# Expert rows of V summed on TensorE through weighted diagonals, rows dealt to two engines stage by stage, and the context projections placed between two choices

## The chip, the cores and the metric

The kernel runs on one core of one Trainium2 chip, in one launch. The metric is the device time in microseconds (us). Its engines here: TensorE (PE, with its weight loads PEld), VectorE (DVE), ScalarE (ACT), GpSimd (POOL) and SyncE (SP), and 16 DMA engines that both SP's and POOL's transfers share. Everything is in float32.

## What is computed

Two blocks follow each other on 256 tokens of width 1024, batch 1. The first has two layers (one with windowed and dilated attention, one with latent attention) and ends in a norm. The second has two layers with a context stream of 256 tokens beside the tokens. Each layer has a mixer (differential attention, a pooling branch, a convolution branch, gates, an output projection) and then a PEER expert layer:

```python
q = (xc @ w_q).reshape(PEER_CHUNK, PEER_HEADS, 2, PEER_HALF)
s = jnp.einsum('thid,hikd->thik', q, sub_keys)
s1, i1 = top_k(s[:, :, 0], 16); s2, i2 = top_k(s[:, :, 1], 16)
cand = s1[..., :, None] + s2[..., None, :]          # 256 candidates per head
top_s, pos = top_k(cand, 16)                         # 16 experts per head, 8 heads
gate = softmax(top_s)
u = u_emb[eidx]                                      # 128 rows of 1024 per token
hid = gelu(einsum('td,thkd->thk', xc, u))
wgt = gate * hid
out = einsum('thk,thkd->td', wgt, v_emb[eidx])
```

For each token 128 experts are chosen, and each needs a row of U (a dot product with the token) and a row of V (summed with a weight). The expert layer runs three times: for the context in layer 0, for the tokens in layer 0, for the tokens in layer 1. In the last layer the context only gives keys and values, so it has no expert layer there.

## The kernel before

Tokens lie on the 128 partitions, in two tiles t = 0, 1. The stages follow each other through `RUN`: run 0 is the context in layer 0, run 1 the tokens in layer 0, run 3 the context in layer 1 (keys and values only), run 2 the tokens in layer 1. The order of work is: `mixer(0)`, the choices of run 0 (`peer_front`), `first_block()` (which needs nothing of run 0), `mixer(1)`, choices of run 1, `mixer(3)`, `mixer(2)`, choices of run 2, end. `mixer(1)` reads the keys and values of the context, which don't depend on run 0's expert layer; `mixer(3)` needs the context after run 0's expert layer; `mixer(2)` needs the tokens after run 1's.

**The rows.** A work item is one expert number k of one tile: POOL issues one indirect DMA (line 974) that fetches for each of the 128 tokens its own row of 1024 floats, 524,288 bytes in all, into one of NG = 8 slots of `ring`. Items are in one fixed order: for each run and tile 128 of U, 128 of V and one with the gate row of the modulation (line 987). Item m waits until item m - 8 was used (`slot_used`). VectorE uses all of them: line 1325 for a U row (multiply with the token, sum into `hid`), lines 1328 and 1331 for a V row (`acc` = row times weight + `acc`, each waiting for the one before), lines 1335 and 1338 for the gate row and the sum into `H`.

**When VectorE takes rows.** `D_` (from line 1340) wraps VectorE's ordinary instructions: after each it adds `PACE[stage]` to an account and takes a row when the account is at 1. `beside(n)` takes `n * PER_PRODUCT[stage]` rows at a place where VectorE is about to wait for TensorE. `expert_rows` takes only rows that may be taken: U rows whose experts are chosen, V rows whose weights are made. `gelu_first` takes the last U rows of a tile and makes the argument of an exp, ScalarE takes the exp (`gelu_exp`, line 1013), `gelu_last` makes the weights. `TURN_AT` says at which place in the stages that is done for run 0: tile 0 after `norm("c")`, tile 1 after the pooling branch of `mixer(1)`.

**A choice.** `choose(r, t, g)` (four groups g for each tile) is 45 VectorE instructions that end in 32 expert numbers for each token (line 1840). `peer_front` of VectorE makes all eight groups of both tiles, then the softmax of the gates. POOL waits for a group's numbers before it fetches its U rows. Only after that do the last rows, weights and sums of both tiles follow.

**TensorE** runs its instructions strictly in the order written: projections (`tokens`, `columns`, line 420 in `sumk`), and `attention`, which goes over units (8 in each layer of the first block, 16 in a mixer), with scores of unit u, then transposed probabilities and values of unit u - 2. Its eight PSUM banks are handed out in rotation by `rot`; in `attention` four are for scores and four rotate. Weights come in blocks of 1 MB (1024 x 256 floats) through `wring`, four slots, fetched by SP (line 937).

## Time and profile before

| | us |
|---|---|
| median of 3 runs | 3917.76 (3910.81 to 3925.49) |
| profiled execution, its own time | 3921.26 |
| span of the profiled execution | 3919.5 |
| busy: PE / DVE / ACT / POOL | 1918.4 / 2800.7 / 402.3 / 1865.8 |

The span runs from the first to the last instruction. Busy time of an engine is the sum of its instructions; its share says nothing about whether the engine sets the end in a stage. A line of a windows view is one stretch of the span with each engine's busy time and count of instructions, the mean clock that TensorE was granted (1.00 is 2.4 GHz, 0.50 is 1.2 GHz), the mean busy share of the 16 DMA engines (it can come out a little above 1) and the gigabytes per second that they moved. Milestones that cut the span into stages: run 0's choices start at about 520, the attention of the first layer lies at 768 to 833, that of the second at 977 to 1033, that of `mixer(1)` at 1244 to 1366, run 1's choices begin at 1742, its last row is added at 2616, `mixer(2)` lasts until 3085, and the rest is run 2's expert layer.

### The profile page before, as it was taken

The page shows a single profiled execution, that of the slowest core. Times are in us where ns is not written, and L with a number is a line of the kernel's source. Part 1 is how long each engine was busy: PE and PEld are TensorE (multiplying, and loading weights), DVE is VectorE, ACT ScalarE, POOL GpSimd, SP SyncE. Part 2 cuts the span into 40 slices and gives each one's busy share as a digit, 9 for nine tenths or more (in the row PEclk, how much of TensorE's full clock was granted, in tenths as well). Part 3 has the DMA queues.
Part 4 walks back from the last instruction along what each step waited for, and adds up shares of the span by engine and source line. Part 5 has one row for each costly group of instructions (what it writes and reads, how often), then busy time and mean ns, then how long its engine had stood idle before and what let it go on. Part 6 is the DMA issues. An engine that isn't in the chain of part 4 may idle for free.

```text
span 3919.5 us, 27161 instructions
## 1 busy us (share of the span) xinstructions
PE 1918.4 (49%) x8842; PEld 1226.2 (31%) x8842; DVE 2800.7 (71%) x4787; ACT 402.3 (10%) x917; POOL 1865.8 (48%) x1556
## 2 busy tenths in 40 slices
PE   6899995386885698790014000029899800000000
PEld 3558484354532346470002000014475700000000
DVE  2322279945869977769997988975411699998898
ACT  1310110023211210010000000002300100000000
POOL 0000023423636766627746777740000377577776
PEclk8999997588786699995557555559999955555555
DMA  6744489967889899979859999963144588699999
GB/s 206 247 172 161 172 285 385 351 233 259 291 313 345 305 352 388 399 249 322 281 172 381 371 355 363 373 243 139 66 149 166 204 290 283 236 378 359 380 374 345
DMA packets 402329, 1111.67 MB, mean 284 GB/s; under 512 B 37139, under 2 KB 91603, under 8 KB 401420
## 3 DMA queue, kind: packets, MB, share of 16 engines
q0 software_dynamic: 223024, 811.71, 56.4%
q1 hardware_dynamic: 179164, 298.22, 21.7%
q8 instruction: 71, 1.16, 0.1%
q14 instruction: 70, 0.57, 0.0%
HBM read 1105.52 MB, written 4.29 MB: 283 GB/s over the span
## 4 chain that ended last, share of the span: by engine, by line
DVE 39%; PE 34%; POOL 12%; issue 8%; DMA 5%; ACT 2%; DVEq 0%; SPq 0%; ACTq 0%; POOLq 0%
PE PS L420 31%; DVE acc L1331 12%; DVE ring L1325 12%; POOL ring L974 12%; DMA wring<-in_w_in 2%; DVE work L1778 1%; DVE work L1775 1%; DVE work L1776 1%; DVE work L1385 1%; DMA ring<-in_peer_u,eidx 1%; ACT work L1001 1%; DVE work L1388 1%; DMA ring<-in_peer_v,eidx 1%; DVE work L1834 1%; DVE work L1837 1%
## 5 line engine op out<-in xcount | busy, mean ns | idle before, releaser
L974 POOL DMA_INDIRECT ring<-in_peer_u,eidx x768 | 955.4, 1244 | 1290.1 <-DVE eidx L1840 516.1
L974 POOL DMA_INDIRECT ring<-in_peer_v,eidx x768 | 900.4, 1172 | 605.0 <-DVE acc L1331 214.1
L1331 DVE SCALAR_TENSOR_TENSOR acc<-ring,small,acc 128x1024 f32<-128x1024 f32 x762 | 977.4, 1283 | 89.6 <-DMA ring<-in_peer_v,eidx 26.5
L1325 DVE SCALAR_TENSOR_TENSOR ring<-ring,xn_peer 128x1024 f32<-128x1024 f32 x768 | 932.5, 1217 | 86.2 <-DMA ring<-in_peer_u,eidx 79.3
L420 PE MATMUL PS<-wring,xnT 128*128 128x512 f32 (+2 forms) x1728 | 743.5, 592 | 22.6 <-issue 17.8
L420 PE MATMUL PS<-xnT,wring 128*128 128x128 f32 (+1 forms) x2896 | 481.9, 329 | 23.6 <-DMA wring<-in_w_in 12.9
L428 PE MATMUL PS<-const,work 128*128 128x128 f32 (+1 forms) x358 | 58.6, 329 | 870.8 <-DVE work L1388 850.8
L420 PEld LDWEIGHTS PS<-wring,xnT 128*128 128x128 f32 x1728 | 332.6, 196 | 426.1 <-issue 418.4
L420 PEld LDWEIGHTS PS<-xnT,wring 128*128 128x128 f32 x2896 | 438.6, 194 | 66.0 <-DMA wring<-in_w_in 14.8
L428 PEld LDWEIGHTS PS<-const,work 128*128 128x128 f32 (+1 forms) x358 | 50.8, 167 | 880.9 <-DVE work L1388 855.1
L1001 ACT ACTIVATE work<-PS 128x512 f32<-128x512 f32 (+5 forms) x377 | 189.0, 525 | 1096.0 <-PE PS L420 774.5
L420 PE MATMUL PS<-wring,work 128*128 128x512 f32 (+2 forms) x640 | 260.3, 567 | 30.4 <-DMA wring<-in_w_out 20.6
L1385 DVE TENSOR_TENSOR work<-work 128x512 f32<-128x512 f32 (+1 forms) x112 | 88.0, 786 | 248.1 <-ACT work L1075 124.6
L420 PEld LDWEIGHTS PS<-wring,work 128*128 128x128 f32 x640 | 123.1, 194 | 163.3 <-issue 144.4
L1385 DVE TENSOR_TENSOR work<-PS,work 128x512 f32<-128x512 f32 x32 | 22.1, 689 | 173.7 <-PE PS L420 147.3
L420 PE MATMUL PS<-work 128*128 128x128 f32 (+1 forms) x512 | 99.9, 358 | 73.2 <-ACT work L1001 73.2
L1385 DVE TENSOR_TENSOR work<-PS,rows 128x512 f32<-128x512 f32 x24 | 16.6, 692 | 160.3 <-PE PS L420 160.2
L491 PE MATMUL PS<-wring,cT 128*32 128x128 f32 x1536 | 69.9, 357 | 99.0 <-issue 99.0
L420 PEld LDWEIGHTS PS<-work 128*128 128x128 f32 x512 | 87.9, 259 | 89.8 <-ACT work L1001 89.8
L1687 DVE TENSOR_REDUCE small<-PS 128x2 f32<-128x1024 f32 (+1 forms) x48 | 50.2, 1045 | 69.9 <-PE PS L671 69.4
L491 PEld LDWEIGHTS PS<-wring,cT 128*32 128x32 f32 x1536 | 61.5, 146 | 109.3 <-issue 109.2
L1013 ACT ACTIVATE small<-small 128x128 f32<-128x128 f32 x6 | 1.9, 311 | 704.5 <-DVE small L1397 704.4
(163 smaller groups left out, 1499.8 us busy)
## 6 DMA issues: line engine op xcount, KB each, us to landing
wring<-in_w_in SPq DMA_DIRECT2D x128, 1024.0 KB, 6.1
wring<-in_w_mod SPq DMA_DIRECT2D x48, 1024.0 KB, 12.4
wring<-in_peer_wq SPq DMA_DIRECT2D x24, 1024.0 KB, 5.2
wring<-in_ab_w_in SPq DMA_DIRECT2D x13, 1024.0 KB, 22.2
wring<-in_conv_out_w SPq DMA_DIRECT2D x12, 1024.0 KB, 5.0
wring<-in_w_out SPq DMA_DIRECT2D x12, 1024.0 KB, 11.2
ring<-in_peer_u,eidx POOLq DMA_INDIRECT x768, 6.2
ring<-in_peer_v,eidx POOLq DMA_INDIRECT x768, 6.1
```

What stands on the lines that cost most here:

```text
L420: ins = pe.matmul(o, a, b, start=(i == 0), stop=(i == n - 1))
L428: ins = pe.transpose(PS[0:width, b, j * P:(j + 1) * P], src[:, (g + j) * width:(g + j + 1) * width], ident)
L491: pe.matmul(strips[j], cT[:, kk, :], w(kk, j * P, (j + 1) * P), start=(kk == 0), stop=False)
L974: pool.indirect_dma_start(ring[:, m % NG, :], None, table, bass.IndirectOffsetOnAxis(ap=eidx[:, r % 2, t, k:k + 1], axis=0))\
L1001: A(act.activation(dst, src, ACT.Copy), *tag)
L1325: v.scalar_tensor_tensor(out=slot, in0=slot, scalar=1.0, in1=xn_peer[:, t, :], op0=ALU.mult, op1=ALU.mult, accum_out=hid[:, k:k + 1]).then ...
L1331: v.scalar_tensor_tensor(out=acc[:, :], in0=slot, scalar=wgt[:, k - NSEL:k - NSEL + 1], in1=acc[:, :], op0=ALU.mult, op1=ALU.add).then_inc ...
L1385: D_(v.tensor_tensor(o, a, b, ALU.mult), *tag)
L1388: D_(v.tensor_tensor(o, a, b, ALU.add), *tag)
L1687: D_(v.tensor_reduce(nmax[:, u % 2, 0:2], PS[:, b:b + 2, 0:nk], AX_X, ALU.max, negate=True))
L1775: D_(v.max_index(idx[:, 0:8], vals[:, 0:8], src))
L1776: D_(v.match_replace(scratch, vals[:, 0:8], src, -3e38))
```

## The change

- 576 of the 768 V rows go to TensorE (`summed`): all of tile 0 in the three runs, and in tile 1 of runs 1 and 2 the rows with k % 4 != 3. VectorE keeps all 768 U rows, all V rows of run 0's tile 1, and one in four of the other tile 1's.
- For each such row ScalarE writes a 128 x 128 matrix `diag` with the tokens' weights on its diagonal (identity times a weight per partition; ND = 5 buffers), and TensorE multiplies it with the row in the ring, two matmuls of 512 columns that accumulate in two PSUM banks (6, 7 for tile 0; 4, 5 for tile 1). `slot_summed` counts them; POOL waits for the one or the other count. In an attention, TensorE sums a unit's rows after the values of unit u - 2 (`sum_rows`), and ScalarE writes their diagonals ahead of that unit's other work (`diags`); in runs 1 and 2 the sums stand after `mixer(3)` and after `peer_front(2)`. In tile 1 of these runs VectorE adds TensorE's sum to `acc` once, before the gate row.
- The order of the items is written out (`ITEMS`): run 0 has V rows of tile 0 in the attention of the first and of the second layer (5 per unit, 40 each) and 48 in that of `mixer(1)` (3 per unit), with 50 and 78 U rows of tile 1 between; in runs 1 and 2 the last 80 V rows of tile 0 alternate with U rows of tile 1.
- The weights of run 0's tile 0 are made before the first attention (`TURN_AT` "ab"), those of its tile 1 before the attention of `mixer(1)` ("heads 1"). `rows_upto` makes VectorE finish rows up to an item at a place; `rows_free` lets it take rows up to an item from there on.
- In runs 1 and 2 tile 0 is chosen, finished with its U rows and weighed before tile 1 is chosen; in run 1 `mixer(3)` stands between the choice of tile 0 and its weights.
- Paces change: "front0" 0.3 to 0.35, "front1" and "front2" 0.5 to 0.35, 16 rows per product in "m3"; none while the second tile of runs 1 and 2 is chosen. The eight rows before the first choice and the rows beside the output projection are gone.
- While TensorE sums, fewer banks rotate: [4, 5] in the attention with sums, six after those of the first block. `hid` and `wgt` get one copy per tile.

```diff
-PACE = {"front0": 0.3, "ab": 0.8, "c": 0.8, "m1": 0.7, "front1": 0.5, "m3": 0.8, "front2": 0.5}
-PER_PRODUCT = {"ab": 6, "c": 6, "m1": 5, "m3": 4}
-BESIDE_QUERIES = 8
+PACE = {"front0": 0.35, "ab": 0.8, "c": 0.8, "m1": 0.7, "m3": 0.8, "front1": 0.35, "front2": 0.35}
+PER_PRODUCT = {"ab": 6, "c": 6, "m1": 5, "m3": 16}
+SUMS_PER_UNIT = {"ab": 5, "c": 5, 1: 3}
+        def items(r, kind, t, first=0, last=NSEL):
+            ITEMS.extend((r, kind, t, k) for k in range(first, last))
+        def both(r, t, first):
+            for k in range(first, NSEL):
+                items(r, "v", 0, k, k + 1)
+                items(r, "u", 1, k - first, k - first + 1)
+            items(r, "u", 1, NSEL - first)
+        a, b = len(range(8)) * SUMS_PER_UNIT["ab"], 16 * SUMS_PER_UNIT["ab"]
+        U1_EARLY = 50
+        items(0, "u", 0)
+        items(0, "v", 0, 0, a)
+        items(0, "u", 1, 0, U1_EARLY)
+        items(0, "v", 0, a, b)
+        items(0, "u", 1, U1_EARLY)
+        items(0, "v", 0, b)
+        items(0, "gate", 0, 0, 1)
+        items(0, "v", 1)
+        items(0, "gate", 1, 0, 1)
+        for r in (1, 2):
+            items(r, "u", 0)
+            items(r, "v", 0, 0, 48)
+            both(r, 1, 48)
+            items(r, "gate", 0, 0, 1)
+            items(r, "v", 1)
+            items(r, "gate", 1, 0, 1)
+        def summed(r, kind, t, k):
+            return kind == "v" and (r > 0 or t == 0) and (t == 0 or k % 4 != 3)
+        PE_ITEMS = [m for m, it in enumerate(ITEMS) if summed(*it)]
+        DVE_ITEMS = [m for m, it in enumerate(ITEMS) if not summed(*it)]
+        ORDER = {m: (summed(*ITEMS[m]), n) for own in (PE_ITEMS, DVE_ITEMS) for n, m in enumerate(own)}
+        PLACE = {it: ORDER[m][1] for m, it in enumerate(ITEMS)}
+        SUMS = {(r, t): [k for k in range(NSEL) if summed(r, "v", t, k)] for r in range(3) for t in range(T)}
+        OWN = {(r, t): [k for k in range(NSEL) if not summed(r, "v", t, k)] for r in range(3) for t in range(T)}
+        def used_wait(m):
+            by_pe, n = ORDER[m]
+            return slot_summed if by_pe else slot_used, n + 1
...
+                state["banks"] = [4, 5] if s in SUMS_PER_UNIT else [4, 5, 6, 7]
                 for u in range(len(units) + 2):
                     if u < len(units):
                         take([2 * (u % 2), 2 * (u % 2) + 1], ("S", s, u))
@@ -470,7 +517,25 @@
                     if u > 1:
                         turns(u - 2)
                         values(u - 2)
-                state["banks"] = 8
+                    if u < len(units):
+                        sum_rows(SUMS_PER_UNIT.get(s, 0))
+                state["banks"] = list(range(6)) if s in ("ab", "c") else list(range(8))
+            def sum_rows(n):
+                for _ in range(n):
+                    m = PE_ITEMS[state["summed"]]
+                    r, _, t, k = ITEMS[m]
+                    b, _ = sums(r, t)
+                    if k == 0:
+                        take([b, b + 1], ("acc", r, t))
+                    pe.wait_ge(*at("diag", r, t, k))
+                    pe.wait_ge(g_landed[m % NG], 16 * (m // NG + 1))
+                    for c in range(2):
+                        ins = pe.matmul(PS[:, b + c, :], diag[:, state["summed"] % ND, :], ring[:, m % NG, 512 * c:512 * c + 512],
+                                        start=(k == SUMS[r, t][0]), stop=(k == SUMS[r, t][-1]))
+                    ins.then_inc(slot_summed, 1)
+                    state["summed"] += 1
...
+            for m, (r, kind, t, k) in enumerate(ITEMS):
+                if m >= NG:
+                    pool.wait_ge(*used_wait(m - NG))
+                if kind == "gate":
                     _, layer, which = modrow(r)
...
+            def diags(n):
+                for _ in range(n):
+                    j = weighted["next"]
+                    r, _, t, k = ITEMS[PE_ITEMS[j]]
+                    if k == 0:
+                        act.wait_ge(*at("weights_of", r, t))
+                    if j >= ND:
+                        act.wait_ge(slot_summed, j - ND + 1)
+                    A(act.activation(diag[:, j % ND, :], ident, ACT.Copy, scale=wgt[:, t, k:k + 1]), "diag", r, t, k)
+                    weighted["next"] += 1
             def root(dst, src, waits, *tag):
                 act.wait_ge(*at(*waits))
...
-            top_exps(1)
+            top_exp(1, 0)
+            mixer(3, [("experts", 1, 0, GROUPS - 1), ("h_peer", 0, T - 1)])
             gelu_exp(1, 0)
-            mixer(3, [("experts", 1, T - 1, GROUPS - 1), ("h_peer", 0, T - 1)])
+            diags(len(SUMS[1, 0]))
+            top_exp(1, 1)
             gelu_exp(1, 1)
+            diags(len(SUMS[1, 1]))
             mixer(2, [("tok", "k", 3, T - 1), ("h_peer", 1, T - 1)])
             peer_front(2)
-            top_exps(2)
             for t in range(T):
...
+                        v.wait_ge(slot_used, j)
+                        total = acc[:, :]
+                        if SUMS[r, t]:
+                            total = sums(r, t)[1]
+                            v.wait_ge(slot_summed, PLACE[r, "v", t, SUMS[r, t][-1]] + 1)
+                        if SUMS[r, t] and OWN[r, t]:
+                            v.tensor_tensor(acc[:, :], acc[:, :], total, ALU.add).then_inc(*step("dve"))
+                            v.wait_ge(L.sem["dve"], L.count["dve"])
+                            total = acc[:, :]
+                        v.tensor_tensor(acc[:, :], total, slot, ALU.mult).then_inc(slot_used, 1)
...
+            def rows_upto(r, kind, t, k):
+                rows_at["upto"] = PLACE[r, kind, t, k] + 1
+                expert_rows(rows_at["upto"] - rows_at["next"])
+                assert rows_at["next"] == rows_at["upto"], (r, kind, t, k, rows_at)
+            def rows_free(r, kind, t, k):
+                rows_at["upto"] = PLACE[r, kind, t, k] + 1
...
+            def weigh(r, t):
+                gelu_first(r, t)
+                top_scale(r, t)
+                gelu_last(r, t)
...
+            mixed_norm(0, [])
+            rows_free(0, "u", 0, NSEL - 1)
+            for t in range(T):
+                choose_tile(0, t, norm_ab)
+            for t in range(T):
+                top_scale(0, t)
             first_block()
             pace("m1")
             mixer(1, [("product", "oT", "c", T - 1, 1)])
             pace("front1")
-            peer_front(1, [("product", "xnT", ("p", 0), T - 1, 1)])
-            expert_rows(2 * NI * T)
+            mixed_norm(1, [("product", "xnT", ("p", 0), T - 1, 1)])
+            rows_upto(0, "gate", 1, 0)
+            rows_free(1, "u", 0, NSEL - 1)
+            choose_tile(1, 0)
+            top_scale(1, 0)
+            pace("m3")
+            mixer(3, [("product", "xnT", ("m", 1), T - 1, 1)])
+            pace(None)
             gelu_first(1, 0)
             gelu_last(1, 0)
-            pace("m3")
-            mixer(3, [("product", "xnT", ("m", 1), T - 1, 1)])
-            expert_rows(NI * T)
-            gelu_first(1, 1)
-            gelu_last(1, 1)
-            expert_rows(NI * T)
-            pace(None)
+            choose_tile(1, 1)
+            weigh(1, 1)
+            rows_upto(1, "gate", 1, 0)
             mixer(2, [("product", "xnT", ("m", 3), T - 1, 1)])
             pace("front2")
-            peer_front(2, [("product", "xnT", ("p", 1), T - 1, 1)])
-            for t in range(T):
-                expert_rows(NI * T)
-                gelu_first(2, t)
-                gelu_last(2, t)
-            expert_rows(NI * T)
+            mixed_norm(2, [("product", "xnT", ("p", 1), T - 1, 1)])
+            rows_free(2, "u", 0, NSEL - 1)
+            choose_tile(2, 0)
+            weigh(2, 0)
+            pace(None)
+            choose_tile(2, 1)
+            weigh(2, 1)
+            rows_upto(2, "gate", 1, 0)
     return L.mark
```

## Rows read from the trace of the kernel before

**Rows 1.** The page's slices, 40 of 98 us; PEclk and DMA in tenths.
```profile
DVE  2322279945869977769997988975411699998898
PEclk8999997588786699995557555559999955555555
DMA  6744489967889899979859999963144588699999
```

**Rows 2.** Windows of five long stages; columns: busy us of each engine (count), clock, DMA share, GB/s.
```profile
0.00:520.00 520.00, 457.92 (x2455) 285.61 (x2456) 139.97 (x297) 84.28 (x204) 6.49 (x14) 0.96 0.55 186
520.00:1742.00 1222.00, 893.89 (x4019) 580.95 (x4018) 953.86 (x1661) 199.45 (x477) 624.36 (x514) 0.80 0.89 326
1742.00:2616.00 874.00, 92.13 (x421) 58.94 (x419) 783.21 (x1293) 25.11 (x42) 624.72 (x514) 0.55 0.89 327
2616.00:3085.00 469.00, 434.89 (x1601) 261.39 (x1601) 158.09 (x274) 84.37 (x180) 0.00 (x0) 0.97 0.36 122
3085.00:3919.50 834.50, 39.53 (x354) 39.34 (x352) 765.60 (x1265) 9.10 (x16) 610.25 (x514) 0.53 0.89 327
```

**Rows 3.** Windows: a V phase, a U phase of run 2, V rows beside mixer(3).
```profile
3371.00:3548.50 177.50, 0.00 (x0) 0.00 (x0) 164.07 (x129) 0.00 (x0) 137.82 (x126) 0.50 0.96 362
3551.00:3731.00 180.00, 0.00 (x0) 0.00 (x0) 157.51 (x257) 0.00 (x0) 141.29 (x128) 0.50 0.98 371
2042.00:2246.00 204.00, 59.98 (x149) 27.38 (x147) 172.92 (x142) 12.21 (x19) 148.09 (x126) 0.64 0.97 365
```

**Rows 4.** Groups by line in that V phase: busy us, mean ns, idle before.
```profile
L1331 DVE SCALAR_TENSOR_TENSOR acc<-ring,small,acc 128x1024 f32<-128x1024 f32 x116 | 149.0, 1284 | 12.1
L974 POOL DMA_INDIRECT ring<-in_peer_v,eidx x115 | 125.4, 1091 | 35.7 <-issue 34.7 <-DVE acc L1331 0.9
```

**Rows 5.** POOL's timeline at the end of the U phase: start, duration, idle before.
```profile
3726.74 0.98 POOL L974 DMA_INDIRECT ring<-in_peer_v,eidx  x1 [0.30 <-issue]
3728.02 0.97 POOL L974 DMA_INDIRECT ring<-in_peer_v,eidx  x1 [0.30 <-issue]
```

**Rows 6.** Windows: one group's choice, the rest of the choices, before a first choice.
```profile
3184.60:3226.10 41.50, 0.00 (x0) 0.00 (x0) 40.71 (x110) 0.00 (x0) 32.47 (x23) 0.50 0.83 281
3226.00:3370.00 144.00, 0.00 (x0) 0.00 (x0) 138.91 (x392) 0.93 (x3) 90.97 (x62) 0.50 0.69 230
1742.00:1754.00 12.00, 12.00 (x110) 12.00 (x109) 11.14 (x32) 1.79 (x3) 0.00 (x1) 1.00 0.65 186
```

**Rows 7.** Groups by line of VectorE in that group's choice.
```profile
L1325 DVE SCALAR_TENSOR_TENSOR ring<-ring,xn_peer 128x1024 f32<-128x1024 f32 x23 | 27.9, 1211 | 0.0
L1325 DVE DVE_READ_ACCUMULATOR ring<-ring,xn_peer 128x1 f32 x23 | 1.9, 83 | 0.0
```

**Rows 8.** TensorE: 64 matmuls of 512 columns at the high clock, from the timeline.
```profile
866.61 27.70 PE L420 MATMUL PS<-wring,work 128*128 128x512 f32 x64 [1.00 <-ACT work L1001]
```

**Rows 9.** Windows: choices, attention, after it, attention, stages, attention, rest of mixer(1).
```profile
520.00:768.00 248.00, 147.84 (x1440) 123.82 (x1438) 233.50 (x657) 19.53 (x43) 100.63 (x106) 0.73 1.02 375
768.00:833.00 65.00, 38.20 (x193) 32.24 (x194) 52.65 (x102) 22.94 (x81) 38.18 (x31) 0.61 1.00 347
833.00:921.00 88.00, 74.14 (x224) 40.14 (x223) 15.33 (x28) 16.23 (x32) 0.94 (x1) 0.94 0.29 98
977.00:1033.00 56.00, 40.74 (x181) 36.13 (x182) 46.44 (x58) 21.24 (x69) 33.24 (x26) 0.62 0.79 257
1033.00:1244.00 211.00, 161.66 (x392) 74.38 (x390) 169.62 (x183) 26.15 (x46) 109.06 (x90) 0.85 0.90 335
1244.00:1366.00 122.00, 71.00 (x240) 41.80 (x240) 118.18 (x232) 35.04 (x94) 95.42 (x73) 0.60 0.89 306
1366.00:1742.00 376.00, 325.35 (x1206) 208.45 (x1206) 273.83 (x342) 35.00 (x58) 211.81 (x163) 0.93 0.94 350
```

**Rows 10.** The same two stages in mixer(2), where no rows run beside.
```profile
2720.00:2780.00 60.00, 45.61 (x234) 26.64 (x235) 45.93 (x93) 34.81 (x93) 0.00 (x0) 0.91 0.04 15
2780.00:3077.00 297.00, 288.41 (x1057) 182.60 (x1057) 61.05 (x97) 30.50 (x53) 0.00 (x0) 1.00 0.42 141
```

**Rows 11.** U rows of VectorE in the choices of run 0 (two records each).
```profile
520.00:768.00 248.00, 119.59 (x197) 0.73 1.02 375
```

**Rows 12.** ScalarE on 128 x 128, from the timeline.
```profile
3731.97 0.31 ACT L1013 ACTIVATE small<-small 128x128 f32<-128x128 f32 x1 [362.75 <-DVE small L1397]
```

More of the change, by code:

```diff
@@ L964, in _ @@
             pool.wait_ge(mod_stored, 64)
-            def rows_in(r, t, table, kinds):
-                for k in range(NSEL):
-                    m = item(r, t, kinds * NSEL + k)
-                    if not kinds and k % (NSEL // GROUPS) == 0:
-                        pool.wait_ge(*at("experts", r, t, k // (NSEL // GROUPS)))
-                    if m >= NG:
-                        pool.wait_ge(slot_used, m - NG + 1)
-                    pool.indirect_dma_start(ring[:, m % NG, :], None, table,
-                                            bass.IndirectOffsetOnAxis(ap=eidx[:, r % 2, t, k:k + 1], axis=0))\
-                        .then_inc(g_landed[m % NG], 16)
-            for r in range(3):
-                for t in range(T):
-                    rows_in(r, t, DR["peer_u_2"].rearrange("l e d -> (l e) d"), 0)
-                    rows_in(r, t, DR["peer_v_2"].rearrange("l e d -> (l e) d"), 1)
-                    m = item(r, t, 2 * NSEL)
-                    pool.wait_ge(slot_used, m - NG + 1)
+            tables = {"u": DR["peer_u_2"].rearrange("l e d -> (l e) d"), "v": DR["peer_v_2"].rearrange("l e d -> (l e) d")}
+            for m, (r, kind, t, k) in enumerate(ITEMS):
+                if m >= NG:
+                    pool.wait_ge(*used_wait(m - NG))
+                if kind == "gate":
                     _, layer, which = modrow(r)
@@ L988, in _ @@
                         .then_inc(g_landed[m % NG], 16)
+                    continue
+                if kind == "u" and k % (NSEL // GROUPS) == 0:
+                    pool.wait_ge(*at("experts", r, t, k // (NSEL // GROUPS)))
+                pool.indirect_dma_start(ring[:, m % NG, :], None, tables[kind],
+                                        bass.IndirectOffsetOnAxis(ap=eidx[:, r % 2, t, k:k + 1], axis=0))\
+                    .then_inc(g_landed[m % NG], 16)
         @block.scalar
@@ L1201, in mixer @@
                     return
+                turn(f"heads {r}")
                 for u in range(len(M_UNITS) + 2):
+                    if u < len(M_UNITS):
+                        diags(SUMS_PER_UNIT.get(r, 0))
                     if r == 0 and u and u % 2 == 0:
@@ L1303, in _ @@
             for t in range(T):
+                top_exp(2, t)
                 gelu_exp(2, t)
+                diags(len(SUMS[2, t]))
+            assert weighted["next"] == len(PE_ITEMS)
         @block.vector
         def _(v):
-            rows_at = {"next": 0, "chosen": 0, "weighted": 0, "pace": 0.0, "due": 0.0, "per_product": 0}
+            rows_at = {"next": 0, "chosen": 0, "weighted": 0, "pace": 0.0, "due": 0.0, "per_product": 0, "upto": len(DVE_ITEMS)}
             def expert_rows(n):
@@ L1315, in expert_rows @@
                 for _ in range(n):
-                    m = rows_at["next"]
-                    if m >= min(rows_at["chosen"], rows_at["weighted"] * NI + NSEL):
+                    j = rows_at["next"]
+                    if j >= rows_at["upto"]:
+                        return
+                    m = DVE_ITEMS[j]
+                    r, kind, t, k = ITEMS[m]
+                    if kind == "u" and j >= rows_at["chosen"] or kind == "v" and r * T + t >= rows_at["weighted"]:
                         return
@@ L1682, in mixer @@
                     return
+                turn_to_v(f"heads {r}")
                 for u in range(len(M_UNITS) + 1):
@@ L1699, in mixer @@
                 v.wait_ge(*at("read", "O", r, len(M_UNITS) - 1))
+                if r == 1:
+                    rows_upto(0, "gate", 0, 0)
+                    rows_free(0, "gate", 1, 0)
                 for t in range(T):
@@ L1784, in mixed_norm @@
                 v.wait_ge(*row_wait(f"m2_{r}"))
+                assert rows_at["next"] > (PLACE[r - 1, "u", 1, NSEL - 1] if r else -1)
                 for t in range(T):
                     for n in range(2):
-                        beside(0.5)
                         v.wait_ge(*at("product", "wo", r, t, n))
@@ L1867, in _ @@
             pace("front0")
-            peer_front(0, [], norm_ab)
+            mixed_norm(0, [])
+            rows_free(0, "u", 0, NSEL - 1)
+            for t in range(T):
+                choose_tile(0, t, norm_ab)
+            for t in range(T):
+                top_scale(0, t)
             first_block()
```

124 lines of the change are left out of this document (66 added, 58 removed).

## The prediction

> **What bounds the kernel now.** I read the slices of the page first, then windows by long stage, then each stage's own. VectorE is busiest in the sum, 2800.7 us, but the slices show three kinds of stage [rows 1]. In `mixer(0)` and `mixer(2)` TensorE works at its high clock and the DMA engines are half idle. In the two long stretches from 1742 to 2616 and from 3085 to the end TensorE is all but idle, VectorE is near full and so are the DMA engines. Between 520 and 1742 all three share the work. The stages last 520, 1222, 874, 469 and 834.5 us [rows 2]; the DMA share is 0.55, 0.89, 0.89, 0.36 and 0.89.
>
> In the row stretches the question is which of three is late: VectorE, POOL that issues, or the transfers. A V phase takes 177.5 us for 128 rows, 1.387 us each, a U phase 180, 1.406 us [rows 3]. In the V phase VectorE's instruction takes 1.284 us with 0.104 (12.1 / 116) before it, its wait on its own last sum; POOL takes 1.091 and 0.30 of issue, which is the same 1.39; the DMA share is 0.96 to 0.98 [rows 3, 4]. So all three run in step there, and the U phase shows that the transfers don't come faster where VectorE could take more: its pair of instructions is 1.211 + 0.083 = 1.294 us [rows 7] against 1.406 spent. I take 1.40 us per row as the price of a row's transfer. Taking V rows from VectorE gives nothing in such a phase. What can be had is the time in which the channel doesn't run full. While VectorE chooses experts, a group of 41.5 us holds 23 rows, one each 1.80 us (share 0.83), and the rest of the choices, after the 128 U rows of tile 0 are used up, falls to 0.69 [rows 6]: V rows can't start, because no weights are made before all choices of both tiles are.
>
> **The change, part by part.** The sum is made against the profiled execution.
>
> *Work moved.* 576 V rows leave VectorE: 576 x 1.39 = 800 us of its time, most of it beside transfers that stay. TensorE gets 1152 matmuls of 512 columns: at the high clock 27.70 / 64 = 0.433 us each [rows 8], 0.87 a row; at the low clock, half of it, twice that, 1.73 a row. The first is under the 1.40 of a transfer, the second over it. ScalarE's diagonal is near 0.31 us [rows 12], bounds 0.31 and 0.60 (a 512-column copy would be the upper neighbour), below 1.40 either way, so hidden; five buffers let it run ahead.
>
> *Run 2, the tail (834.5 us).* VectorE's cost of one group's choice without rows is 41.5 - 23 x 1.294 = 11.7 us [rows 6, 7]. After: 10 us until the first group's numbers (12 in run 1 [rows 6]); three more groups with 45 x 0.35 = 16 rows each, 3 x (11.7 + 16 x 1.294) = 97; 3 for the softmax's shift. By then 48 rows are used and 8 are in the ring. From there the channel runs full: 72 U rows of tile 0 and 386 items behind them, 458 x 1.40 = 641 us. The second choice, 4 x 11.7 = 47 us, lies beside V rows that TensorE sums, and 47 / 1.40 = 34 rows is less than the 48 that stand before the first U row of tile 1. If TensorE is at the low clock there, 27 rows pass instead of 34; that is 7 x 1.40 = 10, of which I take 8. The last tile ends with TensorE's sum added (1.2), gate and add: 5, and the store 4. Sum 10 + 97 + 3 + 641 + 8 + 5 + 4 = 768, so -66 (bounds -25, if a second choice stays as empty as the first, and -77, all that a share of 0.89 leaves to 0.98: 834.5 x 0.09 / 0.98). The two V phases of tile 1 stay at the transfer's pace: three rows of four on TensorE, 5.2 us even at the low clock, against 5.6 for the four transfers.
>
> *Run 1 (874 us).* The same with 12 for the first group and no store, and `mixer(3)` inside: its 60 us of TensorE lay beside V rows before too [rows 3]; its weights are 8 MB, that is 8.4 MB / 0.38 = 22 us of channel. It now lies beside the last U rows of tile 0 (64 of 72 by the two `beside` of 32), whose transfers take 101 us. VectorE's own part of it, two norms and one set of heads, some 25 us, is also beside them. 12 + 97 + 3 + 641 + 22 + 8 + 5 = 788, -86; but the share leaves no more than 874 x 0.09 / 0.98 = 80, so I take -80 (-30 to -86). `mixer(2)` starts only after the last sum, so this counts in full.
>
> *520 to 1742 (1222 us), run 0.* Here the rows are spread beside stages that have their own bounds, so each step is a difference:
> - Choices: 0.35 instead of 0.3 and no V or U row left for the attention. 99 U rows (197 records) were done [rows 11], now all 128 must be before the first attention: 29 x 1.294 = 38 less what the gaps hold, and the channel, already at 1.02 [rows 9], needs as much; with the weights' own 5, +33 (bounds +15, +45).
> - First attention: 65 us with 30 U rows on VectorE. Now 40 V rows: 32 to fetch and 8 of the next kind, 56 us, and what else was loaded, (347 x 65 - 31 x 524) / 380 = 16. I take 77, +12. TensorE's own 38 us at a clock of 0.61 and 40 x 0.87 to 1.73 make 73 to 107 if nothing overlaps: +8 to +42.
> - 833 to 977: 50 U rows instead of 28 V rows, but from the start, where the channel is at 0.29 and VectorE is busy 15 of 88 us [rows 9]. They wait ahead of the gates by six: +5 (0 to +15).
> - Second attention: 56 us, PE 40.7 at 0.62 with 26 rows. With 40 rows on TensorE I take +15 (0 to +50, as the first).
> - 1033 to 1244: 78 rows instead of 90 issued [rows 9]. 12 x 1.40 at a share of 0.90: -10 (-17 to +10; the weights of tile 1 now need its last U row here).
> - Attention of `mixer(1)`: 122 us, VectorE busy 118, 73 rows issued. Without rows the same stage takes 60 in `mixer(2)` [rows 10]. Three sums a unit add 48 x 0.87 = 42 at the high clock and 83 at the low: 102 to 143. TensorE busier than its 71 of 122 should be granted more than 0.60: I take 105, -17 (-20 to +21).
> - Rest of `mixer(1)`: 376 us with 163 rows at a share of 0.94. Some 40 of them are gone, 56 us of channel; TensorE's own need is 297 [rows 10], the channel's 0.94 x 376 - 56 = 297. Both at 297 together give some 328: -48 (-20 to -70). Banks 6 and 7 are asked for while the sum of tile 0 is unread, a few us in it.
> Sum +33 + 12 + 5 + 15 - 10 - 17 - 48 = -10, bounds by these -60 and +90.
>
> *The other stages* (520 and 469 us) hold no rows: 0. One fewer rotation bank pair in the first block's stages costs 0: copies of 0.6 us stand against products of 7.
>
> Total -10 - 80 - 66 = -156. The span of 3919.5 lies in an execution of 3921.3 (1.8 around it), 3.5 over the median of the runs: 3921.3 - 3.5 - 156 = 3762. I predict 3762 us.
>
> **What the skill says against the terms.** The row's transfer at 0.524 MB in 1.40 us is 374 GB/s, and 371 and 375 stand in the windows [rows 3, 9]. The Trainium skill, "DMA: Bandwidth & Descriptors", section "Where 436 GB/s comes from", has 358 GB/s as the bound for what comes from HBM: 1.46 us a row, which the trace already beats, so by that page 916 rows would cost 55 us more, 3817. The same page's table under "Measured (HBM→SBUF, 128 partitions, SWDGE, issued from GpSimd)" has 425 GB/s for one core alone, 1.23 us a row; it speaks for rival B. Of the clock the profile has 0.50 in all stretches with an idle TensorE, 0.64 where it is busy for 29 in 100 and 0.60 at 58 in 100, 1.00 where it is full [rows 3, 9, 10]; "TensorE: Matmul & The Clock Gate", section "HAM oscillation — how this bites in real kernels", says that waits for data between bursts throw it back to the low clock again and again. That is rival C.
>
> **Rivals.**
> A, slower than before: in run 0 TensorE runs in written order, so a V row that hasn't landed holds scores and transposes behind it, and ScalarE can't write the next diagonal, nor take its exps, until the sum is made. If none of the 128 rows in the attentions overlaps with the attention's own chain, they add 128 x 1.40 = 179 us at a full channel and nothing is saved on VectorE there; with the later stages delayed too by half of that (90) and the choices' 45, run 0 is at +314 against -146 from the later runs: about 4086. It decides from a loss of some 150 us in run 0, about half of that price. Against it: five transfers take 7 us and a unit already takes 8 [rows 9], so they fit beside each other.
> B, the gather speeds up once VectorE's chain of sums is gone: POOL shows spacings of 1.28 us (0.98 + 0.30) for a while [rows 5]. 916 rows x 0.12 = 110 us more: 3652. For it: V phases are at exactly VectorE's 1.388. Against: the U phase averages 1.406 with VectorE free for 1.294.
> C, the low clock holds in the phases of sums, with a wait of some 0.2 before each row: 1.9 us for each of the first 48 V rows, 0.5 too many, and 6.0 instead of 5.6 for each of 32 groups of four in tile 1, 2 x (24 + 13) = 74, and 60 from the upper bounds of the attentions: 3762 + 134 = 3896.
> D, only half of the idle channel is won: VectorE's waits on its own instructions are no longer hidden by a row beside them, and the pace of 0.35 leaves rows to later. Runs 1 and 2 give 73 instead of 146: 3835.
>
> **Chances.** Forecast (3720 to 3805) 0.52; B 0.12; C 0.10; D 0.18; A 0.08. The range: the forecast's own, most of D and part of B, 3685 to 3860. Within 0.5% (20 us) is what a measurement of this kernel can't tell from no change. Faster by more: 0.52 + 0.12 + 0.18 and 0.06 of C, 0.88; within: 0.05, the rest of C and a little of A; slower: 0.07, A.
>
> **What the profile after would show.** Right: the tail from the first choice about 768 us with the DMA share 0.95 or more in the second choice (before 0.69 to 0.83); run 1's stretch near 794; a V row's cadence in tile 1 still 1.39 to 1.40; the attention of `mixer(1)` near 105 us. Wrong: a V cadence of 1.27 (B), a clock of 0.50 with PE busy throughout a sum phase and DMA under 0.85 (C), attentions of the first block over 100 us with TensorE waiting for `ring` (A), a second choice with the channel idle (D).

## The result, and the profile after

| | us |
|---|---|
| median before (4 runs beside it) | 3916.49 (3910.81 to 3925.49) |
| median after, 4 runs | 3888.07 (3882.66 to 3892.66) |
| ratio, 95% interval | 0.9925, [0.9902, 0.9948] |
| profiled execution after, its span | 3886.7 |

The change makes the kernel 0.75% faster, 28 us where 156 were forecast, and the time lies above the range (3685 to 3860). The page after, its slices and the groups that changed (columns of the groups: busy us, mean ns, idle before and what ended it):

```profile
PE   6899995369897898899263875698899930587389
PEclk8999997589898899999676998799999975799789
DMA  6754479987768858984889999993144478999999
L535 PE MATMUL PS<-ring,diag 128*128 128x512 f32 x2304 | 1046.1, 603 | 521.8 <-ACT diag L1087 421.7
L1087 ACT ACTIVATE diag<-const,small 128x128 f32<-128x128 f32 x576 | 226.1, 402 | 797.8 <-PE PS L535 785.9
L1420 DVE SCALAR_TENSOR_TENSOR acc<-ring,small,acc 128x1024 f32<-128x1024 f32 x189 | 242.4, 1282 | 277.5 <-DMA ring<-in_peer_v,eidx 271.5
```

The count of the first group tells the error: 576 rows gave 2304 matmul records, four each and not two. Its mean of 603 ns is longer than the pace at which the records follow each other. The timeline of PE in an attention of the changed kernel shows that pace: five rows (20 records) in 8.85 us and one (4 records) in 1.88, some 0.44 to 0.47 us a record:

```profile
819.62 1.88 PE L535 MATMUL PS<-ring,diag 128*128 128x512 f32 x4
821.43 1.13 PE L602 MATMUL PS<-work 64*128 64x256 f32 x8
822.49 8.85 PE L535 MATMUL PS<-ring,diag 128*128 128x512 f32 x20
```

The long stages of the changed kernel as windows (columns as in [rows 2], which they answer to), cut at the same places of the code:

```profile
0.00:520.00 520.00, 458.34 (x2472) 287.80 (x2473) 141.32 (x303) 84.55 (x205) 6.49 (x14) 0.97 0.55 188
520.00:1833.00 1313.00, 1043.02 (x4412) 620.36 (x4410) 810.36 (x1527) 237.30 (x597) 596.07 (x514) 0.89 0.83 302
1833.00:2639.00 806.00, 516.64 (x1420) 237.47 (x1418) 510.22 (x1068) 115.25 (x268) 535.78 (x514) 0.85 0.94 357
2639.00:3108.00 469.00, 432.55 (x1603) 260.86 (x1604) 159.67 (x276) 84.50 (x180) 0.00 (x0) 0.97 0.36 122
3108.00:3886.70 778.70, 447.91 (x1248) 204.25 (x1246) 494.70 (x1042) 98.08 (x240) 531.66 (x514) 0.82 0.93 351
```

Run 0's stretch is 91 us longer (1313 for 1222), run 1's 68 shorter (806 for 874), the tail 56 shorter (778.7 for 834.5). In the stretch that grew, the DMA share fell from 0.89 to 0.83 and TensorE went from 894 to 1043 us at a clock of 0.89. Five of its parts, which answer to [rows 9], are shown (choices, first attention, second attention, attention of `mixer(1)`, rest of `mixer(1)`); the stages between them took 130 us (907 to 1037) and 201 (1138 to 1339):

```profile
520.00:806.00 286.00, 147.12 (x1415) 122.22 (x1413) 264.91 (x710) 19.12 (x41) 140.19 (x132) 0.72 1.00 370
806.00:907.00 101.00, 91.84 (x325) 47.08 (x326) 24.22 (x50) 35.59 (x118) 41.01 (x44) 0.96 0.84 283
1037.00:1138.00 101.00, 94.36 (x349) 53.59 (x348) 19.89 (x34) 38.92 (x121) 36.52 (x39) 1.00 0.68 231
1339.00:1473.00 134.00, 123.11 (x422) 58.47 (x421) 47.97 (x99) 48.30 (x137) 44.12 (x47) 0.99 0.55 177
1473.00:1833.00 360.00, 316.51 (x1121) 199.73 (x1119) 227.35 (x254) 31.57 (x55) 158.06 (x124) 0.94 0.82 305
```

In all three attentions PE is busy for 91 to 93% at a clock of 0.96 to 1.00, VectorE for 20 to 36%, and the DMA share is 0.84, 0.68 and 0.55: TensorE is the bound, not the rows. The waits of the first one say the same from POOL's side (engine and line waiting, for whom, total us, times, longest):

```profile
POOL ring L1047 <- PE PS L535: 58.4, 39, 5.7
ACT diag L1087 <- PE PS L535: 35.4, 29, 1.9
```

In the tail, the second choice, the phase behind it and the last V phase, which answer to [rows 6] and [rows 3]:

```profile
3346.00:3423.00 77.00, 76.39 (x173) 33.86 (x174) 70.88 (x251) 18.44 (x48) 41.23 (x42) 0.97 0.84 294
3423.00:3704.00 281.00, 163.94 (x340) 57.98 (x338) 158.92 (x261) 32.70 (x82) 213.94 (x212) 0.89 1.01 393
3708.00:3880.00 172.00, 168.30 (x384) 73.33 (x384) 44.17 (x36) 37.78 (x96) 120.47 (x122) 0.99 0.98 380
```

The second choice takes 77 us, not 47, and TensorE is busy in all of it with 173 / 4 = 43 rows, 1.73 us each in 75 of the 77. The last V phase is 172 us for 128 rows, 1.34 each, against 1.387 before.

What sets the pace of the phases with nothing but rows is read from POOL, which issues them. In the last V phase its lines are these:

```profile
L1047 POOL DMA_INDIRECT ring<-in_peer_v,eidx x121 | 119.9, 991 | 43.9 <-issue 32.6 <-PE PS L535 9.0 <-DVE acc L1432 2.2
```

It waited 11.2 us for a slot to come free, and for the rest issued one row after another, 0.99 us for the instruction and 0.30 between two, 1.30 in all, with the DMA share at 0.98. So POOL's issuing and the transfers are at their limit together, and no run tells whether the one holds back the other.

### The profile page after: what moved, and what is told of

Its sections match the earlier page's. It is cut to its first block, busy times and chain, and to the rows that moved or that the text cites. A ratio compares the mean times of both kernels' runs of the same rounds, so it can differ in the third digit from the quotient of the medians.

```text
span 3886.7 us, 31785 instructions
## 1 busy us (share of the span) xinstructions
PE 2898.5 (75%) x11146; PEld 1610.7 (41%) x11146; DVE 2116.3 (54%) x4213; ACT 619.7 (16%) x1489; POOL 1670.0 (43%) x1556
## 4 chain that ended last, share of the span: by engine, by line
PE 53%; POOL 14%; DVE 12%; DMA 11%; issue 7%; ACT 2%; SPq 0%; DVEq 0%; ACTq 0%; POOLq 0%
PE PS L467 30%; PE PS L535 19%; POOL ring L1047 14%; DVE ring L1414 5%; DMA ring<-in_peer_u,eidx 3%; DMA ring<-in_peer_v,eidx 3%; DMA wring<-in_w_mod 3%; DMA wring<-in_w_in 2%; ACT work L1062 1%; DVE work L1493 1%; PE PS L556 1%; PE PS L736 1%; DVE work L1891 1%; DVE work L1894 1%; DMA wring<-in_ab_w_in 1%
## 5 line engine op out<-in xcount | busy, mean ns | idle before, releaser
L1047 POOL DMA_INDIRECT ring<-in_peer_u,eidx x768 | 855.9, 1114 | 1541.1 <-DVE work L1891 489.3
L535 PE MATMUL PS<-ring,diag 128*128 128x512 f32 x2304 | 1046.1, 603 | 521.8 <-ACT diag L1087 421.7
L1047 POOL DMA_INDIRECT ring<-in_peer_v,eidx x768 | 804.1, 1047 | 515.5 <-PE PS L535 309.1
L535 PEld LDWEIGHTS PS<-ring,diag 128*128 128x128 f32 x2304 | 426.2, 192 | 1119.4 <-ACT diag L1087 629.3
L467 PE MATMUL PS<-xnT,wring 128*128 128x128 f32 (+1 forms) x2896 | 489.8, 332 | 39.8 <-DMA wring<-in_w_in 24.8
L1420 DVE SCALAR_TENSOR_TENSOR acc<-ring,small,acc 128x1024 f32<-128x1024 f32 x189 | 242.4, 1282 | 277.5 <-DMA ring<-in_peer_v,eidx 271.5
L1087 ACT ACTIVATE diag<-const,small 128x128 f32<-128x128 f32 x576 | 226.1, 402 | 797.8 <-PE PS L535 785.9
L467 PE MATMUL PS<-work 128*128 128x128 f32 (+1 forms) x512 | 72.4, 285 | 46.8 <-ACT work L1062 46.8
```

Source lines behind the costliest of these rows:

```text
L467: ins = pe.matmul(o, a, b, start=(i == 0), stop=(i == n - 1))
L535: ins = pe.matmul(PS[:, b + c, :], diag[:, state["summed"] % ND, :], ring[:, m % NG, 512 * c:512 * c + 512], start=(k == SUMS[r, t][0]), s ...
L1047: pool.indirect_dma_start(ring[:, m % NG, :], None, tables[kind], bass.IndirectOffsetOnAxis(ap=eidx[:, r % 2, t, k:k + 1], axis=0))\
L1087: A(act.activation(diag[:, j % ND, :], ident, ACT.Copy, scale=wgt[:, t, k:k + 1]), "diag", r, t, k)
L1420: v.scalar_tensor_tensor(out=acc[:, :], in0=slot, scalar=wgt[:, t, k:k + 1], in1=acc[:, :], op0=ALU.mult, op1=ALU.add).then_inc(slot_used, 1)
```

## Experiments

Times are medians of one job each with its interval against the runs of the kernel before in that job; three jobs ran on three chips (medians of before 3923, 3909 and 3911).

**Half of TensorE's price.** One of the two matmul calls for each row, two of its four records, except for the first and last row of a tile; what the kernel leaves out is half of the columns of the sums.

```diff
-                    for c in range(2):
+                    for c in range(2 if k in (SUMS[r, t][0], SUMS[r, t][-1]) else 1):
```

> The changed kernel, but of each V row that TensorE sums only the first half of the columns is multiplied (the first and the last row of a tile in full), so the second half of the sums is left out. Theory P (a V row costs TensorE four matmuls of 512 columns, 1.73 us at the high clock, and that lengthens run 0's attentions and holds rows back in the second choices): the two attentions of the first block fall from 101 us each to 70 to 80, that of mixer(1) from 134 to 105 to 115, the second choices let 55 rows pass instead of 44, and the median is 3775 to 3810. Theory W (TensorE stands waiting for the rows' transfers, or for ScalarE's diagonals): the attentions stay within 10 us, the median at 3865 to 3890.

Measured: 3869.25, ratio 0.9853 [0.9811, 0.9895], above the 3775 to 3810 expected. The first numbers of run 1 came at 1752.8, 91 us earlier than in the changed kernel (1844.2), so the stages behind had lost: its last V phase took 184 us, against 172. So I ran it again, on another chip, beside the changed kernel:

> The same kernel as e1_half (of each V row on TensorE only the first half of the columns, the second half of the sums is left out), now beside the changed kernel on one chip. Theory P: first choice of run 1 near 1753 and not 1845, and the whole faster than the changed kernel by that, 80 to 100 us: 3785 to 3815 if the later phases transfer alike. Theory G (what TensorE's price costs before 1845 is given back behind it, as e1_half's 3869 on another chip looks like): within 30 us of the changed kernel.

> The changed kernel unaltered, the measure for g1_half: 3880 to 3945, first choice of run 1 at 1845.

Measured: 3772.69, 0.9665 [0.9621, 0.9709], against 3894.13, 0.9956 [0.9931, 0.9980], for the changed kernel beside it: 121 us, more than the 80 to 100 expected. The windows of g1_half's three attentions:

```profile
801.00:876.00 75.00, 60.96 (x245) 31.71 (x246) 24.13 (x50) 34.70 (x118) 39.29 (x43) 0.92 1.00 359
1007.00:1078.00 71.00, 62.60 (x285) 40.03 (x283) 20.32 (x35) 39.19 (x123) 37.46 (x40) 1.00 0.90 334
1277.00:1373.00 96.00, 84.38 (x332) 41.33 (x330) 48.15 (x99) 47.43 (x138) 44.56 (x48) 0.98 0.76 252
```

And the first expert numbers of run 1, VectorE's timeline, in g1_half:

```profile
1741.69 0.18 DVE L1956 CAST eidx<-work 128x32 int32<-128x32 f32 x1
```

in the kernel as changed:

```profile
1844.18 0.18 DVE L1956 CAST eidx<-work 128x32 int32<-128x32 f32 x1
```

At half the price the attentions take 75, 71 and 96 us (forecast 77, 71, 105), and run 0 ends 12 us earlier than before (1753.5), where -10 was forecast. Theory W falls: ScalarE's diagonals, the code's waits and the rows' transfers were the same, and only the matmuls went. Theory G falls on this chip. Of rival A, a row not landed that holds TensorE, nothing is seen in the changed kernel's attentions: PE's waits there name no transfer of a row, and the channel was emptier than in g1_half, not fuller.

One edit, two chips: beside the kernel before, the half-priced kernel gained 54 us on the first (3923.36 to 3869.25) and 138 on the second (3910.76 to 3772.69). The last section comes back to that.

**Banks.** The kernel before with the change's fewer PSUM banks: `[4, 5]` in the attentions instead of four, six in the first block's stages instead of eight.

> The kernel before with only the PSUM banks of the change: two banks rotate instead of four in the attentions of the first block and of mixer(1), six instead of eight in the stages behind those of the first block. Theory P: within 10 us of before in each attention, median 3905 to 3930. Theory B (the fewer banks lengthen the attentions by holding a transpose until VectorE has read a value): the first block's attentions 15 us or more longer each, 3945 or more.

Measured: 3925.17, 0.9999 [0.9978, 1.0020]; the attentions 62.5, 56 and 123 us for 65, 56 and 122. Theory B falls, and the banks cost nothing, as taken.

**Run 0 as before, runs 1 and 2 as changed.**

```diff
-            return kind == "v" and (r > 0 or t == 0) and (t == 0 or k % 4 != 3)
+            return kind == "v" and r > 0 and (t == 0 or k % 4 != 3)
-SUMS_PER_UNIT = {"ab": 5, "c": 5, 1: 3}
+SUMS_PER_UNIT = {}
-TURN_AT = {"ab": (0, 0), "heads 1": (0, 1)}
+TURN_AT = {"c": (0, 0), "pooled 1": (0, 1)}
+        for t in range(T):
+            items(0, "u", t)
+            items(0, "v", t)
+            items(0, "gate", t, 0, 1)
...
```

> Run 0 as in the kernel before (all its V rows on VectorE, its order, paces and places), runs 1 and 2 as changed. Theory P, with the losses all in run 0 (+91 us until the first choice of run 1) and the gains in runs 1 and 2 (67 and 55): 3917 - 122, 3785 to 3805. Theory S (the stages are coupled, part of run 1's gain comes from rows that run 0 had finished early): 3820 to 3860.

> As e2_run0, but all V rows of runs 1 and 2 stay on VectorE too, which takes them at a pace of 0.5 during the second choice: the new order alone, no row on TensorE. Theory T (TensorE is needed, since only with it a row passes without VectorE's time in the second choice): a second choice takes 47 us plus some 90 rows of 1.39, 172 us for 126 us of transfers, 40 to 50 us lost in each run against e2_run0; median 3875 to 3895. Theory O (the order alone brings the gain): within 20 us of e2_run0.

Measured: 4181.39, 1.0633 [1.0587, 1.0680], and 4219.06, 1.0734 [1.0689, 1.0779]. Both were spoilt by my edit: after a tile's weights VectorE was not allowed any row of run 0 until the next forced place, and the first numbers of run 1 came at 2071, not at 1753.5. They say one thing: where rows are only taken at forced places, run 0 is 318 us longer. Mended (`rows_free(0, "gate", 1, 0)` after the weights of run 0):

> As e2_run0, which by an oversight took no rows of run 0 between its weights and the last stages; now VectorE is free to take them as in the kernel before. Theory P (all the loss in run 0, gains of 38 and 12 in runs 1 and 2 on the chip of e2_run0, 67 and 55 by the first profile of the changed kernel): 3790 to 3870, first choice of run 1 at 1745 to 1765 as before. Theory S (coupled stages): first choice of run 1 as before, but no gain behind it.

> The changed kernel again, unaltered, beside the others, as the measure for them. In its first profile the rows of the last V phase passed at 1.32 us each, while in e1_half and e2_run0, whose code for the last expert layer is the same or does less, they took 1.40. Theory X (the transfers' pace differs between executions or chips, whatever the kernel): tail from its first choice to the end 764 to 810, median 3880 to 3945, and rows of the last V phase at 1.32 to 1.40. Theory Y (the pace comes from the kernel: TensorE at 1.73 us a row holds the issue back just so far that the channel runs evenly): 1.32 again, median 3880 to 3895.

Measured: f2_run0 3805.97, 0.9724 [0.9688, 0.9759]; f1_after 3892.84, 0.9952 [0.9929, 0.9976]. The stages of f2_run0:

```profile
520.00:1740.00 1220.00, 889.47 (x4035) 576.80 (x4034) 953.98 (x1654) 199.85 (x477) 624.02 (x513) 0.82 0.90 327
1740.00:2546.50 806.50, 502.92 (x1271) 221.33 (x1270) 511.51 (x1070) 112.88 (x264) 546.46 (x514) 0.84 0.94 352
3013.00:3809.50 796.50, 449.54 (x1254) 205.37 (x1252) 495.36 (x1044) 98.03 (x240) 563.50 (x514) 0.82 0.93 343
```

Run 0's stretch is 1220 us, for 1222 before; run 1 keeps its 806. The tail is 796.5 us here and 778.7 in the changed kernel, by the phase that the last section takes up. The loss was in run 0 alone, and this version beats both kernels: 87 us under the changed one beside it, 103 under the one before. Run again on the third chip:

> f2_run0 unaltered, the measure for g3_second: 3795 to 3830, with the first choice of run 1 at 1750 to 1760.

Measured: 3795.63, 0.9726 [0.9677, 0.9775]; the first numbers of run 1 came at 1762.8, a little later than the 1750 to 1760 expected.

**Order without TensorE.** f2_run0 with all V rows on VectorE (`summed` returns False), which takes rows at a pace of 0.5 in the second choices.

> As f2_run0, with all V rows on VectorE: the order of runs 1 and 2 alone, mended as f2_run0. From e3_order's later stages (846 and 820 us for 862 and 820): 3890 to 3910. If TensorE's sums are what gains, f2_run0 is 30 to 40 us faster or more; if the order is, they are within 15 us.

Measured: 3873.09, 0.9903 [0.9868, 0.9938], faster than the 3890 to 3910 expected. So of the 103 us, 36 come from the order with this pace and 67 from TensorE's sums. Its second choice in the tail and its last V phase:

```profile
3294.00:3466.00 172.00, 0.00 (x0) 0.00 (x0) 168.66 (x365) 0.00 (x0) 93.00 (x91) 0.50 0.84 282
3687.00:3867.00 180.00, 0.00 (x0) 0.00 (x0) 165.86 (x130) 0.00 (x0) 133.56 (x122) 0.50 0.95 357
```

VectorE alone needs 172 us for a choice and 91 rows, as worked out in the expectation; theory O falls: the two are 67 us apart, and not within 15.

**The share in tile 1.** f2_run0 with `k % 2 == 1` instead of `k % 4 != 3` in tile 1.

> As f2_run0, but in tile 1 of runs 1 and 2 TensorE sums every second V row instead of three of four. Theory P (at 1.73 us a row three of four, 5.2 us in four transfers of 5.3 to 5.6, leave TensorE busy 98% and set the pace of that phase): 2 to 10 us faster than f2_run0, the V phases of tile 1 at 165 us or less. Theory C (the channel sets it): within 3 us of f2_run0 and 170 to 180 us.

Measured: 3807.13, 0.9735 [0.9699, 0.9772], the same as f2_run0. POOL's issues of a V phase of tile 1 spread over 170 us in run 1 and 181 in run 2, for 173 and 172 in f2_run0. TensorE, 98% busy there, was not what set the pace: the same follows from g1_half, where PE's busy time in the last V phase fell from 167 to 110 us and the phase only from 172 to 167. Theory P falls for this phase.

**Filling the second choice.** f2_run0; one V row in four of tile 0 stays on VectorE, at a pace of 0.11 in the second choice, and U rows of tile 1 begin behind 64 V rows.

> As f2_run0; besides, in tile 0 of runs 1 and 2 one V row in four stays on VectorE, which takes it during the second choice (pace 0.11), and U rows of tile 1 start behind 64 V rows instead of 48. Theory P (44 rows pass in a second choice of 77 us because TensorE needs 1.73 us for each, so 19 us of the channel are lost in each run): the second choice takes 90 to 105 us with 65 to 77 rows, 10 to 30 us faster than f2_run0, 3775 to 3800. Rival (the row on VectorE costs the choice as much as the channel wins): within 8 us of f2_run0.

Measured: 3810.71 (3784.26 to 3834.96), 0.9741 [0.9678, 0.9803], against 3795.63: unclear. The second choice and the phase behind it in the tail, g3_second:

```profile
3285.00:3388.00 103.00, 93.00 (x208) 38.74 (x206) 86.31 (x248) 21.03 (x53) 73.89 (x69) 0.98 0.96 356
3388.00:3656.00 268.00, 101.90 (x171) 36.48 (x172) 179.95 (x283) 16.93 (x44) 207.39 (x187) 0.73 0.97 363
```

and g4_run0:

```profile
3256.00:3337.00 81.00, 76.14 (x173) 33.70 (x174) 74.46 (x264) 18.75 (x48) 43.63 (x45) 0.94 0.85 301
3337.00:3620.00 283.00, 165.65 (x343) 58.81 (x342) 164.56 (x273) 34.62 (x88) 213.84 (x215) 0.89 1.01 398
```

The choice was filled as meant, 69 issues at a share of 0.96 for 45 at 0.85. Then the phase behind it ran at 363 GB/s instead of 398, and the sum of both is 371 us for 364. The profiled execution of g3_second is the slowest of its four (3834.96), and it was 8 us behind already at the first numbers of run 1 (1770.9 for 1762.8), and up to there the two kernels do the same. What sets that pace is open (below), so whether filling pays is too.

## Why the prediction was wrong

**The step that failed** is the first of the sum: "TensorE gets 1152 matmuls of 512 columns: at the high clock 27.70 / 64 = 0.433 us each [rows 8], 0.87 a row". The 0.433 is right, and it is the price of one *record*. The code behind that row is `sumk` over 8 k for two halves of the columns and two tiles, 32 calls, and the row has 64 records: a float32 matmul leaves two. I counted calls of the change and took the price of records. A row costs 4 x 0.433 = 1.73 us at the high clock, over the transfer's 1.40, not under it. The row alone could have told: [rows 8] has x64 for what is 32 calls in the kernel's code.

Point by point, against the forecast:

| step | forecast | after | g1_half (price 0.87) |
|---|---|---|---|
| until the first attention | +33 | +38 | +33 |
| first attention | +12 | +36 | +10 |
| stages | +5 | -14 | -13 |
| second attention | +15 | +45 | +15 |
| stages | -10 | -10 | -12 |
| attention of `mixer(1)` | -17 | +12 | -26 |
| rest until run 1's first experts | -48 | -16 | -19 |
| run 0 in all | -10 | +91 | -12 |

With the price as I had it, the model holds on that chip: g1_half's run 0, and its whole, 138 us under the kernel before where 156 were forecast (3773 against 3762; part of this nearness is that the kernel before ran 7 us faster there). The size of the mistake in time is the 121 us between it and the changed kernel on one chip. In the two profiled executions, which lie 138 us apart, 105 of them (1847.1 - 1741.7, the first numbers of run 1 in g2_after and g1_half) are in run 0.

The bounds of these terms (+42, +50, +21) held what was measured, since I had put the low clock's 1.73 there. The sum's upper bound did not: the upper bounds of the seven steps add up to +163, and I wrote +90, just under the +91 that came. Rival C's 3896 is only 8 us from the result, by luck: its clock was wrong in the attentions (0.96 to 1.00, where it wanted the low one), and 74 of its 134 us were to come from runs 1 and 2, which together fell only 22 short of the forecast.

**Rest of `mixer(1)`**: wrong even at the right price. I took channel and TensorE as evenly mixed, 297 us of either in 328. VectorE took the 128 V rows at once and the channel was full until the last one; the chain of waits of the changed kernel has stretches of TensorE behind weights there:

```profile
1589.98 28.19 DMA wring<-in_w_in
1618.22 10.03 PE PS L467 x32
1628.27 38.87 DMA wring<-in_w_in
```

These waits are only a part. In all of the 360 us PE waited 26.4 us for weights (1.8 in the stage of [rows 10], and 30.0 in this stage of the kernel before), and its own busy time was 316.5 us at a clock of 0.94, not 288.4 at 1.00. After 1727 the rows were over and the channel was half empty to the end of the stage:

```profile
1727.00:1833.00 106.00, 102.00 (x432) 60.84 (x430) 28.26 (x62) 15.10 (x28) 0.00 (x0) 1.00 0.48 169
```

**Run 1 (-80 forecast, -68) and the tail (-66, -56)** came nearly as reckoned, but partly because two errors are of opposite sign, which is luck. The second choice took 77 us for 47. My 11.7 us for a group's choice was too low: I subtracted 23 x 1.294 us of rows from 41.5, but records of VectorE overlap where they follow each other: in that window those of the rows last 29.8 us in sum and those of the choice itself 18.1 (64 records), in a busy time of 40.7. The latter last 72.0 / 4 = 18.0 us a group in the second choice of the changed kernel, where no row stands in the gaps. That is most of the 30 us; the engine stood idle for 6 of the 77, so rival D's reason, waits that a row no longer hides, was real but small. TensorE filled the stretch with 43 rows instead of my 34. Against it, row phases ran at 1.32 to 1.34 us a row instead of 1.40 where VectorE's chain of sums was gone: rival B was right in kind and gave half to two thirds of its 0.12, on this chip.

**The rules weighed in the prediction.** 358 GB/s as a bound from HBM ("DMA: Bandwidth & Descriptors", "Where 436 GB/s comes from" in the Trainium skill): windows of 393 and 398 GB/s in phases of nothing but rows beat it. The 425 of the same page was not reached either. The clock: in the three attentions PE was busy for 91 to 93% and was granted 0.96 to 1.00. The section "HAM oscillation — how this bites in real kernels" of "TensorE: Matmul & The Clock Gate" (the Trainium skill) tells of bursts of matmuls that are shorter than the wait for data behind each. The attentions are no such case, so they say nothing against it. Nearer to it are the phases of alternating rows, where PE waits for most rows. In the tail of the changed kernel it was granted 0.89 there, in g1_half, with half of the records, 0.58:

```profile
3330.00:3595.00 265.00, 141.04 (x152) 34.67 (x152) 152.99 (x251) 28.30 (x71) 204.03 (x202) 0.58 1.02 397
```

So waits between bursts can bring the low clock in this program, and need not. In g1_half it cost nothing that shows: the phase took 265 us for 281.

## What to carry to other kernels

Count an operation's cost in the records that the trace has for one call, not in calls: divide the count of a row by the calls of the code behind it before a duration is used. Work moved to an idle engine is free only in the stages where that engine is idle; here the same move gave 67 us in two stretches and, with its order, took 91 in a third, and dealing it by stage gave 2.7% instead of 0.75%. An instruction's cost from a mixed window is not the window less the sum of its neighbours' records, where records overlap. In `mixer(1)` the rows filled the channel first and left it half empty behind; that spreading them over the stage would have gained is likely, but no run tested it.

## What the runs showed of the hardware

A gather of 524,288 bytes has no one pace. In one execution of the changed kernel (f1_after) the two like phases, second tile's U rows with V rows on TensorE, ran so in run 1 and in run 2:

```profile
2190.00:2484.00 294.00, 160.41 (x326) 57.00 (x325) 161.54 (x267) 32.72 (x84) 225.30 (x210) 0.87 0.99 375
3446.00:3722.00 276.00, 161.14 (x334) 56.79 (x332) 161.91 (x268) 32.58 (x83) 207.59 (x213) 0.89 1.02 402
```

1.40 us per row in one, 1.30 in the other, with PE, VectorE and ScalarE busy for the same time. POOL was not: its instruction took longer, and only for V rows (the U rows' took 0.98 and 0.99 us). The lines of its V rows in the two phases:

```profile
L1047 POOL DMA_INDIRECT ring<-in_peer_v,eidx x84 | 102.0, 1214 | 28.3 <-PE PS L535 21.3 <-issue 7.0
L1047 POOL DMA_INDIRECT ring<-in_peer_v,eidx x85 | 81.6, 960 | 27.3 <-issue 24.1 <-PE PS L535 3.3
```

84 times 0.25 us is 21 us, more than the difference of 18. In f2_run0 it is the phase of run 2 that is slow (300 us) with V rows at 1.22 us of POOL, so it does not belong to the rows that one run reads. Whether POOL's instruction held the transfers back or they it, is not shown.

The other difference is between chips. The same half-priced kernel had a median of 3869.25 on one and 3772.69 on another, and the four executions on each lie within 14 us. Its last V phase, in e1_half and in g1_half:

```profile
3673.00:3857.00 184.00, 118.17 (x196) 35.21 (x196) 48.40 (x45) 37.86 (x97) 125.12 (x126) 0.90 0.96 365
3601.00:3768.00 167.00, 110.04 (x195) 31.47 (x193) 44.08 (x35) 36.53 (x91) 118.61 (x122) 0.96 0.98 385
```

In e2_run0, on the chip of e1_half, that phase took 183 us. So theory Y falls, though f1_after by itself came out as it said (3892.84, and 1.32 in the last V phase). Of theory X it is left that the pace differs with the same kernel, between chips and within one execution; the cause was not found. It moved the half-priced kernel by 97 us. The kernel before hardly shows it (3909 to 3923 on the three chips), perhaps because its V phases were at VectorE's 1.387 anyway. So what the change and f2_run0 earn holds for the chips that they ran on, and on the chip of e1_half neither was measured.

ScalarE's 128 x 128 scaled copy took 402 ns, where I had taken 0.31 us, and was hidden: apart from the first diagonal of a tile, whose weights had to be made, PE waited for diagonals for some 5 us in each phase of alternating rows, and in the attentions not at all.
